# Hybrid decoder trunk: inverting four blocks level by level in three pairs of PSUM banks, with one burst of projections behind each level

## What is computed

```python
lower = jnp.where(strict, jnp.einsum('bhncd,bhnsd->bhncs', k_beta, k) * decay, 0.0)
t_mat = jnp.eye(C, dtype=jnp.float32) + lower
u = lax.linalg.triangular_solve(t_mat, v_beta, left_side=True, lower=True, unit_diagonal=True)
w = lax.linalg.triangular_solve(t_mat, k_beta * jnp.exp(g_cum)[..., None], ...)
```

## Time and profile before

| | |
|---|---|
| Median of 3 runs | 2107.09 us (2105.57 to 2109.25) |
| Profiled execution, its own time | 2105.42 us |
| its span | 2103.5 us |
| granted TensorE clock, mean | 0.999 |
| busy: PE / DVE / ACT / POOL | 99% / 49% / 37% / 18% |

### The profile page before, as it was taken

How to read it: one execution, slowest core, us unless ns; L and a number is a source line. 1 busy time by engine, 2 the same in 40 slices (tenths; PEclk the granted TensorE clock), 3 DMA queues, 4 the chain that set the end, 5 groups by cost and what they waited for, 6 DMA issues and landing times.

```text
span 2103.5 us, 31665 instructions
## 1 busy us (share of the span) xinstructions
PE 2078.7 (99%) x13097; PEld 1679.5 (80%) x13097; DVE 1027.0 (49%) x1391; ACT 775.4 (37%) x1058; POOL 380.1 (18%) x343
## 2 busy tenths in 40 slices
PE   9999999999999999999999999999999999999999
PEld 7888888877777888888888888887777778888887
DVE  5433333688765643433343433336887655334322
ACT  5222222465555422222232222224755554222211
POOL 1110011105034501001111010121051345111000
PEclk9999999999999999999999999999999999999999
DMA  5222222322120322222222222223212112222222
GB/s 195 86 97 100 95 91 95 123 82 79 55 79 21 103 97 100 100 95 90 98 99 100 100 100 93 93 102 115 81 63 92 41 44 97 100 100 89 94 103 75
DMA packets 30645, 192.40 MB, mean 91 GB/s; under 512 B 3216, under 2 KB 5392, under 8 KB 11984
## 3 DMA queue, kind: packets, MB, share of 16 engines
q1 hardware_dynamic: 30160, 189.80, 26.2%
q10 hardware_dynamic: 384, 1.14, 0.1%
HBM read 188.70 MB, written 2.10 MB: 91 GB/s over the span
## 4 chain that ended last, share of the span: by engine, by line
PE 86%; DVE 8%; ACT 4%; issue 1%; POOL 1%; DMA 0%; SPq 0%; DVEq 0%; ACTq 0%; POOLq 0%
PE psum L989 27%; PE psum L991 26%; PE psum L990 26%; DVE wl L1900 1%; PE psum L1460 1%; PE psum L1445 1%; PE psum L1414 1%; ACT wh L1528 1%; PE psum L1305 1%; PE psum L1302 1%; DVE acc L1983 1%; DVE wrk L1998 1%; DVE XL L1915 1%; DVE m L1996 1%; DVE gkT L2012 0%
## 5 line engine op out<-in xcount | busy, mean ns | idle before, releaser
L989 PE MATMUL psum<-XH,wh 128*128 128x512 f32 x1904 | 755.3, 397 | 10.9 <-DVE wl L1900 3.9
L991 PE MATMUL psum<-XH,wl 128*128 128x512 f32 x1904 | 742.2, 390 | 0.0
L990 PE MATMUL psum<-XL,wh 128*128 128x512 f32 x1904 | 742.1, 390 | 0.0
L989 PEld LDWEIGHTS psum<-XH,wh 128*128 128x128 f32 x1904 | 357.6, 188 | 107.5 <-issue 23.5
L991 PEld LDWEIGHTS psum<-XH,wl 128*128 128x128 f32 x1904 | 357.7, 188 | 75.9
L990 PEld LDWEIGHTS psum<-XL,wh 128*128 128x128 f32 x1904 | 358.0, 188 | 71.3 <-issue 1.0
L1908 DVE TENSOR_TENSOR wl<-raw,wh 128x2048 fp32r<-128x2048 f32 x88 | 201.7, 2292 | 159.4 <-ACT wh L1533 159.4
L989 PE MATMUL psum<-HH,wh 128*128 128x512 f32 x704 | 273.9, 389 | 0.0
L990 PE MATMUL psum<-HL,wh 128*128 128x512 f32 x704 | 273.9, 389 | 0.0
L991 PE MATMUL psum<-HH,wl 128*128 128x512 f32 x704 | 273.9, 389 | 0.0
L1528 ACT ACTIVATE wh<-raw 128x2048 fp32r<-128x2048 f32 (+1 forms) x88 | 161.7, 1837 | 303.6 <-PE psum L991 303.5
(11 more groups left out here) (255 smaller groups left out, 1940.2 us busy)
## 6 DMA issues: line engine op xcount, KB each, us to landing
raw<-weights SPq DMA_DIRECT2D x143, 1024.0 KB, 4.8
raw<-weights SPq DMA_DIRECT2D x32, 896.0 KB, 4.4
xT<-xt SPq DMA_DIRECT2D x4, 512.0 KB, 6.3
memT<-memt SPq DMA_DIRECT2D x2, 1024.0 KB, 4.7
out<-xT SPq DMA_DIRECT2D x8, 256.0 KB, 6.1
stripsA<-strip_table SPq DMA_DIRECT2D x2, 768.0 KB, 6.8
raw<-weights SPq DMA_DIRECT2D x2, 512.0 KB, 6.6
stripsB<-strip_table SPq DMA_DIRECT2D x2, 512.0 KB, 6.9
```

Source lines behind the costliest of these rows:

```text
L989: pe.matmul(out_ap, a_hi, b_hi, start=first, stop=False)
L990: pe.matmul(out_ap, a_hi, b_lo, start=False, stop=False)
L991: return pe.matmul(out_ap, a_lo, b_hi, start=False, stop=last)
```

## The change

The steps `t`, `n`, `w` now belong to one block, and INVERSION is a list of eight levels of four steps each: `t` of blocks 0 to 3, level 0 of blocks 0 to 3, and so on, `w` last. Banks 2 and 3 come in as a third pair: blocks 0 and 3 share the pair at 4, and blocks 1 and 2 have those at 6 and 2, or at 2 and 6 in the levels behind which sums of squares use banks 2 and 3 (`t`, `n` 3, `w`). Behind each level stand the entries of BEHIND_LEVEL in the order written there, the rounds of selection of ROUNDS_BEHIND, and one `pull(3.6, False)`, which gives 6, 5, 5, 6, 5, 5, 5 and 6 rounds of projections with their evictions and, but for dk 1, no followers. The second half of `lo 12` moves up to directly behind the first half, ahead of `t`. One round less is left for `u` (1 instead of 2), and `ap 13` moves from behind `w` to behind the first step of the recurrence.

```diff
 LEVELS = 6
-INVERSION = [("rows",), ("decay", 0), ("decay", 1), ("kq", 0), ("kq", 1), ("decay", 2), ("decay", 3), ("kq", 2), ("kq", 3)]
-for _g in range(2):
-    INVERSION += [("t", _g)] + [("n", _g, _j) for _j in range(LEVELS)] + [("w", _g)]
-SELECTING = [s for s in INVERSION[:9] if s != ("kq", 2)] + [s for s in INVERSION[9:] if s[0] != "t"]
+SETUP = [("rows",), ("decay", 0), ("decay", 1), ("kq", 0), ("kq", 1), ("decay", 2), ("decay", 3), ("kq", 2), ("kq", 3)]
+INVERSION = [[("t", _b) for _b in range(NB)]] + [[("n", _j, _b) for _b in range(NB)] for _j in range(LEVELS)]
+INVERSION += [[("w", _b) for _b in range(NB)]]
+SUMS_BEHIND = {0: 9, 4: 11, 7: 13}
+INVERSION_BANK = {s: (4, 2, 6, 4)[i] if lv in SUMS_BEHIND else (4, 6, 2, 4)[i]
+                  for lv, steps in enumerate(INVERSION) for i, s in enumerate(steps)}
+BEHIND_LEVEL = ((("hs", 9), ("rs", 8), ("rs", 9)),
+                (("ap", 8), ("ap", 9), ("sq", 10)),
+                (),
+                (("sq", 11), ("hi", 13, 0, KD), ("lo", 13, 0, KD // 2)),
+                (("hs", 11), ("rs", 10), ("rs", 11), ("lo", 13, KD // 2, KD)),
+                (("ap", 10), ("ap", 11), ("sq", 12)),
+                (("sq", 13), ("hi", 14, 0, KD), ("lo", 14, 0, KD // 2)),
+                (("hs", 13), ("rs", 12), ("rs", 13), ("lo", 14, KD // 2, KD)))
+ROUNDS_BEHIND = (2, 1, 3, 2, 2, 1, 2, 1)
...
 RECURRENCE = [("u",)]
```

```diff
-    def pull(target):
+    def pull(target, follow=True):
...
             if k == KD - 1:
                 order.append(("ev", gi))
+                if not follow and (name, c) != ("dk", 1):
+                    continue
...
-    for i, step in enumerate(INVERSION):
+    for i, step in enumerate(SETUP):
         order.append(step)
-        if step in SELECTING:
+        if step != ("kq", 2):
             sel(1)
-        if i < 9:
-            pull(0.7 if i < 6 else 1.3)
-        else:
-            pull(1.78)
+        pull(0.7 if i < 6 else 1.3)
         if i == 0:
             put(("vt", 2), ("vt", 3))
+    for x in [x for _, x in later if x[0] == "lo"]:
+        order.append(x)
+    later.clear()
+    for steps, events, n in zip(INVERSION, BEHIND_LEVEL, ROUNDS_BEHIND):
+        put(*steps)
+        put(*events)
+        sel(n)
+        pull(3.6, False)
+    later += [(0, ("ap", 12)), (1, ("ap", 13))]
+    later.sort(key=lambda x: x[0])
```

The counters follow the new order (`nth`), POOL's EGr step stands at level 1 of block 0, and the sums of squares wait for the copy of the block that used banks 2 and 3:

```diff
-    return 2 * LEVELS * (b // 2) + 2 * j + b % 2 + 1
...
+    return NB * j + b + 1
...
-                        elif kind == "n" and at_ == (0, 1):
+                        elif kind == "n" and at_ == (1, 0):
...
-                            if nj == 9:
-                                pe.wait_ge(S["v_done"], NB)
+                            if nj == SUMS_BEHIND[0]:
+                                pe.wait_ge(S["n_done"], of("n_done", last_on(2, 0)[1] + 1))
+                            elif nj == SUMS_BEHIND[4]:
+                                pe.wait_ge(S["n_done"], of("n_done", nth(last_on(2, 4)[2], 4)))
+                            elif nj == SUMS_BEHIND[7]:
+                                pe.wait_ge(S["w_done"], of("w_done", last_on(2, 7)[1] + 1))
```

TensorE's `t`, `n` and `w` keep their matmuls and wait for the last user of their bank pair (`emptied` looks it up in INVERSION_BANK):

```diff
+                            b, = at_
+                            pb = INVERSION_BANK["t", b]
+                            pe.wait_ge(S["start_done"], of("start_done", NB + 2 * b + 1))
+                            if b == 3:
+                                pe.wait_ge(S["n_done"], of("n_done", emptied(("t", b))[1] + 1))
+                            elif pb == 2:
+                                pe.wait_ge(S["v_done"], NB)
+                                pe.wait_ge(S["nq_r"], 8)
+                            else:
+                                pe.wait_ge(S["lt_done"], of("lt_done", 3 if pb == 4 else 4))
...
+                            j, b = at_
+                            pb = INVERSION_BANK["n", j, b]
+                            before = emptied(("n", j, b))
+                            if before[0] == "t":
+                                pe.wait_ge(S["n_done"], of("n_done", before[1] + 1))
+                            elif before[1] < LEVELS - 1:
+                                pe.wait_ge(S["n_done"], of("n_done", nth(before[2], before[1] + 1)))
+                            else:
+                                pe.wait_ge(S["x_done"], of("x_done", before[2] + 1))
+                            if pb == 2 and j in SUMS_BEHIND:
+                                pe.wait_ge(S["nq_r"], SUMS_BEHIND[j] + 1)
+                            pe.wait_ge(S["n_done"], of("n_done", nth(b, j)))
+                            if j:
+                                pe.wait_ge(S["f_done"], of("f_done", nth(b, j - 1)))
+                            else:
+                                pe.wait_ge(S["start_done"], of("start_done", NB + 2 * b + 2))
...
+                            pb = INVERSION_BANK["w", b]
+                            before = emptied(("w", b))
+                            if before[0] == "n":
+                                pe.wait_ge(S["x_done"], of("x_done", before[2] + 1))
+                            else:
+                                pe.wait_ge(S["w_done"], of("w_done", before[1] + 1))
+                            pe.wait_ge(S["x_done"], of("x_done", b + 1))
```

More of the change, by code:

```diff
@@ L127, with emptied, last_on @@
 LEVELS = 6
-INVERSION = [("rows",), ("decay", 0), ("decay", 1), ("kq", 0), ("kq", 1), ("decay", 2), ("decay", 3), ("kq", 2), ("kq", 3)]
-for _g in range(2):
-    INVERSION += [("t", _g)] + [("n", _g, _j) for _j in range(LEVELS)] + [("w", _g)]
-SELECTING = [s for s in INVERSION[:9] if s != ("kq", 2)] + [s for s in INVERSION[9:] if s[0] != "t"]
+SETUP = [("rows",), ("decay", 0), ("decay", 1), ("kq", 0), ("kq", 1), ("decay", 2), ("decay", 3), ("kq", 2), ("kq", 3)]
[13 more added lines that the diff above has]
+ROUNDS_BEHIND = (2, 1, 3, 2, 2, 1, 2, 1)
+def emptied(step):
+    level = [s for steps in INVERSION for s in steps]
+    bank, last = INVERSION_BANK[step], None
+    for s in level[:level.index(step)]:
+        if INVERSION_BANK[s] == bank:
+            last = s
+    return last
+def last_on(bank, level):
+    return [s for s in INVERSION[level] if INVERSION_BANK[s] == bank][-1]
 RECURRENCE = [("u",)]
@@ L446, in nth @@
 def nth(b, j):
-    return 2 * LEVELS * (b // 2) + 2 * j + b % 2 + 1
-def nth_f(b, j):
-    return nth(b, j) - 2 * (b // 2)
-def nth_ps(b, step):
-    return 2 * (LEVELS + 1) * (b // 2) + 2 * step + b % 2 + 1
+    return NB * j + b + 1
 def row_half(par, ch, j):
@@ new lines, in gdn @@
+                            act.wait_ge(S["n_ps"], of("n_ps", nth(b, 0)))
+                            if b == 0:
+                                act.wait_ge(S["kq_ps"], of("kq_ps", NB))
+                            for ch in range(2):
+                                ins = act.activation(NN[rows[ch], b].rearrange("p h c -> p (h c)"),
+                                                     bank[INVERSION_BANK["t", b] + ch][rows[ch], 0:WB], ACT.Copy)
+                            ins.then_inc(S["n_done"], 1)
```

130 lines of the change are left out of this document (48 added, 82 removed).

## The result

The changed kernel takes 2114.79 us (median of 9 runs) against 2107.09 (9 runs): the ratio is 1.0036 with an interval of 1.0027 to 1.0045, slower by 0.36%. Eight of its runs lie between 2110.55 and 2116.74 us; the ninth took 4183.61 us and is left out of the ratio. The forecast was no change, 2107.3. The profiled execution took 2115.82 us for a span of 2114.0, 10.4 us more than the span before, while the medians differ by 7.7: what follows explains this pair of profiles, and some 2.7 us of it are not in the typical run.

A forecast was written before the change was run, and what follows sets the result against it. TensorE, busy 2078.7 of 2103.5 us, bounds the kernel. Saved turns against two new waits gave 61.0 against 60.6 us a layer, less 0.3 in the recurrence: +0.1 a layer, +0.2 in all, 2107.3 us; range 2102.5 to 2111.0.

The forecast's parts named there:

- The turns: TensorE's switches between inversion blocks and projection bursts: 0.36 us a pair; 16 bursts become 8, saving 2.9 us a layer.
- the sums of squares: Eight matmul instructions behind `w`, 0.87 us; the same term is added to `t` and level 3.
- The wait for U: TensorE idle 0.70 us behind the last dk 2 matmul; two v rounds there would cut it to about 0.2.
- The wait of the fourth `t`: Ahead of `t` of block 3, TensorE waits 1.8 us for POOL's LT, which ends at 510.46.
- rival C: DVE keeps the ports it shares with POOL, so LT ends later: 2109.7 us, +0.12%; chance 0.10.
- The wait of the fourth block of level 3: Block 3 waits for block 0's copies, FT being 2.3 us late because DVE's "lo 13" stands behind ACT's "hi 13".
- Rival D: The level 3 wait isn't there: 2102.7 us, or 2099 with the `t` wait gone too; chance 0.15 for either.
- Rival E: The turns don't get shorter, 0.36 not being paid per burst: +5.8, 2113 us; no chance beyond B's 0.10.
- levels 0, 1, 4: 4 x 0.70 + ... = 6.64 each: Inversion levels: four blocks at 0.70 us, 0.15 turn, 0.04 wait and five projection rounds of 3.65 make 6.64 us each.
- rival B: Half-speed clock behind both new waits, four events at 1.6 us: 2113.7; chance 0.10 for three or more, 0.15 one or two.
- gain in the recurrences: Behind `u`, two v rounds instead of one fill TensorE's idle time: 0 to 0.53 us back a layer, 0.3 taken.
- just in time: Behind level 1, DVE's 7.6 us of work ends as FT of block 0 is due, 0.99 after level 2's start.

The follow-up runs named there:

- the shift: Changed kernel with block 3's 24 kq matmuls done twice, into the same places: 2116.03 us (one run); the kernel before with the same edit: 2108.15 us, ratio 1.0007.
- kernels with breaks: Changed kernel, some with other mends too, with projections put in the middle of inversion levels: 2116.34, 2112.13, 2109.03 (half-burst breaks), 2105.99, 2106.42, 2106.36 us (single-round breaks).
- the last two kernels: Kernel with single-round breaks, one selection round moved from behind level 1 to level 0, level 4's break or all four behind the third block: 2106.42 and 2106.36 us.

## Why the prediction was wrong

**Right, within 0.2 us:** what the change removes. The turns are 0.36 us a pair, the sums of squares 0.87, rounds 0.69. The wait for U fell from 0.70 to 0.19. *The wait of the fourth `t`*: forecast 1.8, measured 1.68 in both layers, and the row of POOL behind it:

```profile
509.06 1.97 POOL L907 TENSOR_TENSOR LT<-LT,cst 128x384 f32<-128x384 f32 x1
```

It ends 3.94 us after the first `t`, where the working had 3.96 from the earlier trace rows: POOL does get in between, and rival C is out. *The wait of the fourth block of level 3*: forecast 2.3, measured 2.17 and 2.19, and the experiment that moves "hi 13" removes it. Rival D is out. Rival E too, by the busy time of layer 1.

**The step that failed** is "levels 0, 1, 4: 4 x 0.70 + ... = 6.64 each". The 0.70 us of a block was read where two blocks stand in a row and used for four. Taken that way a level step has only work and semaphores in it. Three of the twelve level steps of levels 0 to 5 ran out of instructions and took 1.11, 1.11 and 1.37 us more, 3.6 us in all. No rival of mine held it, and where the measured 2114.8 comes near the times of rivals B (2113.7) and E (2113), it is by chance. A rival for the gaps was in reach: the page before lists the queue of instruction packets, in the trace before they set out no closer than 3.4 us in this stretch, and a rate of 384 instructions in 2.8 us against that would have given it a price.

**The second error is what rival B left out.** Its price was right: level 3 of layer 0 took 1.66 us more than its term at half clock (an estimate of 1.6), and one event had its chance inside the range. But there were four half-rate stretches in the profile of the changed kernel and one in that of the kernel before, and only one of the four stood at the waits that B listed; the others are at the start and in the attention stages, where the change touches nothing and the sum had no term. What they cost depends on what follows. In the kernel before, layer 0, the half rate from 611.34 costs nothing: the next wait for `wl` shrinks by as much. Single rows of three timelines, each the wait for the `wl` of the attention stage's last split, in the kernel before (layer 0, behind the half rate), before (layer 1, at full rate) and after (layer 0):

```profile
615.52 0.50 PE L989 MATMUL psum<-XH,wh 128*128 128x512 f32 x1 [0.32 <-DVE wl L1900]
...
1660.77 0.50 PE L989 MATMUL psum<-XH,wh 128*128 128x512 f32 x1 [1.83 <-DVE wl L1900]
```

```profile
619.34 0.72 PE L1014 MATMUL psum<-XH,wh 128*128 128x512 f32 x1 [1.82 <-DVE wl L1939]
```

After the change the full wait of 1.82 comes first and the half rate behind it, in both layers: 1.4 to 1.6 us each. The thirteen profiles sort themselves by it. From the first v matmul of layer 1 to the end they take 490.9 to 491.2 us where the half rate falls ahead of that wait or not at all (nine) and 492.5 to 492.6 where it falls behind it (four, the changed kernel's among them).

The sum then: 3.6 us of issue gaps, 1.6 of half rate in level 3, 0.7 of smaller misses (level 2 and `w`, 0.2 each a layer), 4.0 outside the stretch (0.6, 1.4 and 1.4 measured, where I had counted 0.6 of gain in the recurrences), and 0.3 because layer 1 of the kernel before takes 60.3 us from t to v and not 60.6, which the prediction took for both layers: 10.2 us, the whole difference between 0.2 forecast and 10.4 measured in this pair of profiles. The miss in level 2 is where the prediction had DVE "just in time": FT of block 0 starts 1.22 us after that level's start (532.69 against 531.47) and not 0.99.

**Open.** That a gap stands at the end of a block of 256 instructions and ends 2.2 to 2.9 us after a packet's start is shown in all 24 cases and by the shift; that it comes where a block is used up faster than the next one arrives is what the 22 dense blocks and the comparison of levels of four and of two blocks bear out, though I made no kernel in which only the packets' times differ. The five gaps at 20662 in kernels with breaks are the exception: their blocks took 4.1 to 5.1 us, and it is the late packet that stands out. With the count of instructions the places could have been worked out from the code; I did not do so before any run. Not known is why that packet sets out late, 1.8 to 2.7 us into its block, and what lets one dense block through without a gap. Between a packet's start and the gap TensorE ran 40 to 88 matmuls (six, and part of the break, in the last two kernels). Why 2 us of idle are followed by the half rate in some executions and not in others stays open too: of the ten waits of about 2 us in level 3 (five profiles, two layers), five were.

## What to carry to other kernels

A duration read in a short run of small instructions isn't valid for a run twice as long. Count the instructions of a dense stretch, weight loads and semaphore waits included: here a block of 256 of them took at least about 2.9 us with one exception, and 18 of the 22 blocks that would have run in 1.87 us stood still for the rest. Breaking such a stretch with a little slow work cured most of the gaps, not all; the break should be short, since whatever other engines have queued behind the stretch needs the long burst for cover. And a wait on which several things converge hides a second cause: remove it and see what stands there next.

## What was unexpected of the hardware

- TensorE ran out of instructions while all its semaphores were open: gaps of 0.5 to 1.7 us between the starts of two matmuls, always 2.19 to 2.88 us after a 16 KB packet of its instruction queue had started, at some 140 small instructions a microsecond (384 in 2.8 us), and always at the end of a block of 256 instructions: from one such end to the next it took 2.85 us or more in this stretch, with one exception (1.87) in thirteen profiles. The packet itself took 0.96 us (that of 518.07). The Trainium skill (Runtime: NRT & Kernel Launch, "Instruction fetch mechanics") says that the sequencer streams 16 KiB blocks by itself and that the cost of crossing one is mostly hidden. The size of the blocks agrees with the packets here (0.02 MB); the cost does not: in the changed kernel it shows in three of sixteen steps of a level or of `t` and `w`.
- A half-rate stretch lost 1.7 us of clock (4.00 us at 0.57 in the window from 544.00), wherever it fell, and cost between nothing and 1.6 us of time, by whether a wait that TensorE would have had anyway came behind it. The Trainium skill (TensorE: Matmul & The Clock Gate, "What's actually happening") has the half rate as the state that too little activity brings back. Each such stretch here had an idle time of TensorE ahead of it; the converse fails, since after 2.19 us of idle in level 3 of layer 1 the clock stayed at 1.00.
- POOL, with two DVE instructions queued against its second LT step, took 1.97 us instead of 1.00, in both layers. It ended while the second of the two was running (the pair took from 508.91 to 512.11, POOL's LT step ended at 511.03), so POOL was let in between; its end came within 0.02 us of the forecast.
